# The half swaps of the rotary embedding: their transfers issued by GpSimd instead of ScalarE

## The chip, the cores and the metric

The kernel runs on one core of one Trainium2 chip. Time is the device time of one execution in microseconds (us). The engines named here are TensorE (PE, matrix products; PEld is its weight load), VectorE (DVE, elementwise work and reductions), ScalarE (ACT, activations and copies), GpSimd (POOL) and SyncE (SP, which here only issues DMAs). Each engine runs its own list of instructions in order; semaphores tie the lists together. A DMA is issued from an engine's list and moves its data afterwards, on 16 DMA engines that all queues share.

## The reference

Two pre-norm layers over 512 tokens of width 1024, all in float32, and a final RMSNorm. Each layer projects the normalised input to 23 chunks of 128 columns and feeds them to two groups of heads:

```
h = rmsnorm(x, g); z = h @ w_in
u_lru, g_lru, q, g_nsa, kc, vc, ks, vs, kwn, vwn, gate_logits = split(z)
y_lru = rg_lru(causal_depthwise_conv(u_lru))               # gated linear recurrence over the tokens
o_cmp = cmp_attention(q, compress(kc), compress(vc))       # compressed branch, q not rotated
q_rot = apply_rope(q)
o_slc = slc_attention(q_rot, apply_rope(ks), vs)           # selected blocks (here all 8 of them)
o_win = win_attention(q_rot, apply_rope(kwn), vwn)
y = [y_lru * silu(g_lru), (gated sum of the three o) * silu(g_nsa)]
x = x + y @ w_out

def apply_rope(t):                                          # per head of 64: halves x1, x2 of 32
    return concat(x1*cos - x2*sin, x2*cos + x1*sin)
```

`apply_rope` needs, beside each row of a chunk, the row of the other half of its head.

## The kernel before

Everything is kept transposed: a chunk of a projection is a tile of 128 columns (partitions) by 512 tokens. A weight chunk is loaded by SP into one of four `stage` slots, split by ACT into a high part `w_hi` (L774) and by DVE into a low part `w_lo` (L983), and PE multiplies it in 8 pieces of three matmuls (L1351 to L1353) into one of three PSUM banks. DVE takes the bank out, times `rstd`, into one of six slots of `E` (step EV: L1032, for q chunks L1029).

The order of all steps of a layer is written out in `schedule()`, and each engine walks through that one list and does its own part of each step, so it is the order on every engine. Six chunks of a layer are rotated: ks, kw and q0 to q3. For each the list has

- SWAP: four DMAs (L837) copy blocks of 32 partitions of the chunk in `E` into the slot `n % 2` of `swp` with the two halves of each head exchanged. ACT issues them; it first waits for EV of that chunk, and for the rotation two chunks earlier to be done with the slot. In the second layer the first of them also waits until the squares of the norm, which use `swp` too, are added up.
- ROPE: DVE waits until all four have landed, then multiplies `swp` by `sinT` (L1217), `E` by `cosT` (L1218) and adds them (L1219).
- RHI and LOW: ACT copies the result to `q_st` or `k_st` (L895), DVE stores the remainder (L1229).

For the q chunks the order on DVE is EV q(n), then the low part of a weight chunk, `cmpb` (CMPE, L1205, of the chunk before), ROPE q(n), and right behind it EV q(n+1). On PE the step CMP (L1576, scores of the compressed branch) of q(n) stands in the middle of the projection of chunk n+1 and waits for EV q(n); after q3 the step TURN (L1568) of the gate chunk waits in the same manner for the EV of `gate`, which stands behind ROPE q3.

GpSimd builds constants in the first 4 us, computes roots (L749, L762), and adds the squares between the layers (L738, L741); it has nothing to do while the chunks are projected.

Of the kernel before, what the change touches and what calls it, by code (L numbers as in the profile page):

```python
# [35 lines left out]
KT = D_MODEL // P  # L36
# [13 lines left out]
N_STAGE, N_RING, N_PT, N_E, N_SWP = 4, 3, 3, 6, 2  # L50
# [326 lines left out]
def hybrid_trunk(nc, x, norm_g, w_in, conv_w, conv_b, lru_wa, lru_ba, lru_wi, lru_bi, lru_lambda,  # L377
# [3 lines left out]
    plan = Plan(sched)  # L381
    split_no, load_no, z_no, aux_no, e_no = plan.split_no, plan.load_no, plan.z_no, plan.aux_no, plan.e_no
    rope_no, unit_no, turn_no, data_no, group_no = plan.rope_no, plan.unit_no, plan.turn_no, plan.data_no, plan.group_no

    ctx = ExitStack()
    with ctx:
        def sb(name, shape, dt=F32):
            return ctx.enter_context(nc.sbuf_tensor(name, shape, dt))

        def sem(name):  # L390
            return ctx.enter_context(nc.semaphore(name))
# [20 lines left out]
        swp = sb("swp", [P, N_SWP, SEQ])  # L412
# [48 lines left out]
        z_full, z_dve = sem("z_full"), sem("z_dve")  # L461
# [10 lines left out]
        squared, sq_added, root_ok, diag_ok = sem("squared"), sem("sq_added"), sem("root_ok"), sem("diag_ok")  # L472
# [6 lines left out]
        rot_ok, rope_hi, rope_lo, swapped = sem("rot_ok"), sem("rope_hi"), sem("rope_lo"), sem("swapped")  # L479
# [31 lines left out]
        def e_slot(key):  # L511
            return E[:, e_no[key] % N_E, :]
# [186 lines left out]
        @block.gpsimd  # L699
        def _(pool):  # L700
            links = [0]

            def link(ins):

                links[0] += 1
                ins.then_inc(pool_link, 1)
                pool.wait_ge(pool_link, links[0])

            link(pool.memset(ident[:, :], 0.0))
            link(pool.affine_select(out=ident[:, :], in_=ident[:, :], compare_op=ALU.not_equal, fill=1.0,  # L710
                                    base=0, pattern=[[-1, P]], channel_multiplier=1))
            pool.memset(ones[:, :], 1.0).then_inc(first_consts, 1)
            pool.tensor_copy(ident_b[:, :], ident[:, :]).then_inc(consts, 1)
            pool.tensor_tensor(fold[:, :], ident[:, 0:NCOL], ident[:, NCOL:2 * NCOL], ALU.add).then_inc(consts, 1)
            link(pool.memset(causal_b[:, :], 0.0))

            pool.affine_select(out=causal_b[:, :], in_=causal_b[:, :], compare_op=ALU.is_ge, fill=BIG, base=0,
                               pattern=[[-1, P]], channel_multiplier=1).then_inc(consts, 1)
            link(pool.memset(mask_c[:, :, :], 0.0))

            pool.affine_select(out=mask_c[:, :, :], in_=mask_c[:, :, :], compare_op=ALU.is_ge, fill=BIG,
                               base=-(CMP_LEN - 1), pattern=[[P, TT], [-CMP_STRIDE, NC]],
                               channel_multiplier=1).then_inc(consts, 1)
            link(pool.memset(row_ok[:, :], 1.0))

            pool.affine_select(out=row_ok[:, :], in_=row_ok[:, :], compare_op=ALU.is_ge, fill=0.0,
                               base=-(CMP_LEN - 1), pattern=[[P, TT]], channel_multiplier=1).then_inc(consts, 1)
            pool.memset(kc_bd[:, :], 0.0).then_inc(consts, 1)
            pool.memset(mhalf[:, :], -0.5).then_inc(consts, 1)
            pool.memset(upad[:, 0:CONV_W - 1], 0.0).then_inc(consts, 1)  # L730
            pool.wait_ge(consts, N_CONST)

            def add_square(tag, m):

                n = tag * KT + m
                pool.wait_ge(squared, n + 1)
                if m == 0:
                    pool.tensor_copy(sq_acc, sq_tmp).then_inc(sq_added, 1)  # L738
                else:
                    pool.wait_ge(sq_added, n)  # L740
                    pool.tensor_tensor(sq_acc, sq_acc, sq_tmp, ALU.add).then_inc(sq_added, 1)  # L741

            def root(tag):

                if tag < 0:
                    pool.wait_ge(x_mean, 1)
                else:
                    pool.wait_ge(a_dve, plan.freed(plan.aux, aux_no[("ss", tag)])[1])
                pool.tensor_tensor(rt[:, :], ms[:, :], mhalf[:, :], ALU.pow).then_inc(root_ok, 1)  # L749

            root(-1)
            for st in sched:
                kind = st[0]
                if kind == "ON":
                    for m in (2 * st[2], 2 * st[2] + 1):
                        add_square(st[1], m)
                elif kind == "NORM":
                    root(st[1])
                elif kind == "FMEAN":
                    t = st[2]  # L760
                    pool.wait_ge(fin_mean, t + 1)
                    pool.tensor_tensor(fin_rt[:, t:t + 1], fin_ms[:, t:t + 1], mhalf[:, 0:1], ALU.pow).then_inc(fin_root, 1)  # L762

        @block.scalar
        def _(act):
# [24 lines left out]
            def evicted(l, name):  # L790
                act.wait_ge(z_dve, plan.freed(plan.z, z_no[("Z", l, name)])[1])
# [19 lines left out]
            for st in sched:  # L811
                kind = st[0]
# [11 lines left out]
                if kind == "TANH":  # L824
                    _, l, name = st
                    evicted(l, name)
                    act.activation(silu_g[:, int(name[-1]), :], e_slot((l, name)), ACT.Tanh, scale=0.5).then_inc(gate_tanh, 1)
                elif kind == "SWAP":
                    _, l, name = st
                    n = rope_no[(l, name)]  # L830
                    evicted(l, name)
                    if n >= N_SWP:
                        act.wait_ge(rot_ok, n - N_SWP + 1)
                    if name == "ks" and l >= 1:
                        act.wait_ge(sq_added, KT * l)
                    for a in range(4):
                        act.dma_start(swp[32 * a:32 * a + 32, n % N_SWP, :],  # L837
                                      e_slot((l, name))[32 * (a ^ 1):32 * (a ^ 1) + 32, :]).then_inc(swapped, 16)
                elif kind == "GATES":
                    _, l, t = st  # L840
                    n = CT * l + t
# [16 lines left out]
                elif kind == "SQRT":  # L858
                    _, l, half = st
# [3 lines left out]
                elif kind == "YH" and st[2] == "n":  # L863
                    _, l, _, i = st
# [4 lines left out]
                elif kind == "YH":  # L869
                    _, l, t = st  # L870
# [4 lines left out]
                elif kind == "FLAT":  # L875
                    _, l, kv = st
# [9 lines left out]
                elif kind == "RHI":  # L886
                    _, l, name = st
# [9 lines left out]
                elif kind == "TURNE":  # L897
                    _, l, name = st
# [12 lines left out]
                elif kind == "S":  # L911
                    _, l, unit, r = st
# [11 lines left out]
                    for g in range(N_KV):  # L924
                        n, j = 4 * u + 2 * r + g, 2 * g + r
# [4 lines left out]
                elif kind == "T":  # L930
                    key = (st[1], *st[2])
                    if key[1] != "B" and data_no[key] % 2 == 0:
                        n, d, rows = turn_no[key], data_no[key], P if key[1] == "P" else NC
# [4 lines left out]
                    elif key[1] == "B":  # L938
                        l, _, i, b = key
# [11 lines left out]
                elif kind == "GE":  # L951
                    _, l, t, c = st
# [664 lines left out]
```

## Time and profile before

| | us |
|---|---|
| median of 3 runs | 629.15 (627.08 to 630.05) |
| the profiled execution: its own time | 629.98 |
| the profiled execution: span from first to last instruction | 628.3 |
| PE busy | 584.3 (93%) |
| DVE busy | 402.6 (64%) |
| ACT busy | 294.1 (47%) |
| POOL busy | 16.0 (3%) |

The 1.7 us between span and time lie outside the recorded instructions. The mean granted clock of TensorE is 0.985 of full speed. Issuing a DMA isn't counted as busy, though the engine's list stands still for it: 48 swap transfers are issued by ACT at 0.61 us each, about 29 us of its list. The first layer projects from about 12 to 150 us, the second from about 335 to 460 us; between and behind them PE works on attention and on the output projection.

### The profile page before, as it was taken

What the parts mean: (1) busy time and instruction counts of PE and PEld (TensorE: products, weight loads), DVE (VectorE), ACT (ScalarE), POOL (GpSimd) and SP (SyncE); (2) the same over time, 40 slices, a digit from 0 to 9 for tenths busy, and PEclk for the clock granted to TensorE, in tenths of its full rate; (3) what the DMA queues carried; (4) which work ended last, traced back from release to release, by engine and by line L of the source; (5) the groups of instructions that cost most, each with busy time, mean ns of one, the idle gap of its engine ahead of it and who ended that gap; (6) DMA issues with size and microseconds to landing.
All of it is one profiled execution on the core that took longest, in us unless ns stands there. A gap on an engine that the chain in (4) does not pass through costs nothing.

```text
span 628.3 us, 8688 instructions
## 1 busy us (share of the span) xinstructions
PE 584.3 (93%) x3207; PEld 409.1 (65%) x3207; DVE 402.6 (64%) x690; ACT 294.1 (47%) x586; POOL 16.0 (3%) x32
## 2 busy tenths in 40 slices
PE   4999999889999989998999999999899999999994
PEld 3776777667556555555788677777776666555563
DVE  4786966776555664755576679667664766557532
ACT  3647654424444452543453574462344545445522
POOL 1000000000000000000230000000000000000000
PEclk9999999998999998999899999998999999999999
DMA  8755393343111110101232745734421112000112
GB/s 243 201 155 152 87 231 85 84 102 104 56 34 34 34 35 1 34 0 35 67 101 70 198 122 145 142 82 99 110 74 35 34 39 64 0 2 1 34 34 68
DMA packets 94889, 50.71 MB, mean 81 GB/s; under 512 B 42992, under 2 KB 92288, under 8 KB 94848
## 3 DMA queue, kind: packets, MB, share of 16 engines
q1 hardware_dynamic: 91456, 45.95, 28.9%
q10 hardware_dynamic: 3392, 4.21, 2.5%
q8 instruction: 26, 0.43, 0.3%
q14 instruction: 15, 0.12, 0.1%
HBM read 44.90 MB, written 2.10 MB: 75 GB/s over the span
## 4 chain that ended last, share of the span: by engine, by line
PE 65%; DVE 13%; ACT 8%; DMA 5%; issue 5%; ACTq 2%; POOLq 0%; POOL 0%; DVEq 0%
PE z_ps L1351 10%; PE z_ps L1353 9%; PE z_ps L1352 9%; PE s_ps L1410 6%; PE t_ps L1426 5%; PE a_ps L1462 5%; DMA swp<-E 4%; PE o_ps L1462 3%; ACTq L837 2%; PE o_ps L1351 2%; PE o_ps L1352 2%; PE o_ps L1353 2%; ACT probs L928 2%; PE s_ps L1413 2%; DVE w_lo L983 2%
## 5 line engine op out<-in xcount | busy, mean ns | idle before, releaser
L1351 PE MATMUL z_ps<-h_hi,w_hi 128*128 128x512 f32 x264 | 111.1, 421 | 3.1 <-DVE h_lo L976 2.2
L928 ACT ACTIVATE probs<-s_ps,mn 128x128 f32<-128x128 f32 (+3 forms) x128 | 66.3, 523 | 99.7 <-DVE mn L1259 87.5
L1353 PE MATMUL z_ps<-h_hi,w_lo 128*128 128x512 f32 x264 | 103.6, 393 | 0.0
L1352 PE MATMUL z_ps<-h_lo,w_hi 128*128 128x512 f32 x264 | 103.6, 392 | 0.0
L774 ACT ACTIVATE w_hi<-stage 128x1024 fp32r<-128x1024 f32 x58 | 61.0, 1054 | 74.2 <-PE z_ps L1353 44.8
L1259 DVE TENSOR_REDUCE mn<-s_ps 128x1 f32<-128x128 f32 (+3 forms) x128 | 56.8, 485 | 52.0 <-PE s_ps L1413 51.9
L983 DVE TENSOR_TENSOR w_lo<-stage,w_hi 128x1024 fp32r<-128x1024 f32 x58 | 71.1, 1226 | 11.1 <-ACT w_hi L774 10.0
L1351 PEld LDWEIGHTS z_ps<-h_hi,w_hi 128*128 128x128 f32 x264 | 49.9, 189 | 22.4 <-issue 14.5
L1353 PEld LDWEIGHTS z_ps<-h_hi,w_lo 128*128 128x128 f32 x264 | 49.8, 189 | 11.1
L1267 DVE COPY probsT<-t_ps 128x512 f32<-128x512 f32 (+1 forms) x48 | 32.9, 686 | 36.1 <-PE t_ps L1426 24.8
L1352 PEld LDWEIGHTS z_ps<-h_lo,w_hi 128*128 128x128 f32 x264 | 50.1, 190 | 7.9 <-issue 0.2
L1410 PE MATMUL s_ps<-k_st,q_st 64*128 64x128 f32 (+3 forms) x384 | 47.2, 351 | 3.5 <-ACT probs L928 3.4
L1426 PE MATMUL t_ps<-ident,probs 128*128 128x128 f32 x320 | 49.3, 280 | 0.3 <-ACT probs L928 0.2
L1426 PEld LDWEIGHTS t_ps<-ident,probs 128*128 128x128 f32 x320 | 36.0, 141 | 15.3 <-issue 11.9
L1410 PEld LDWEIGHTS s_ps<-k_st,q_st 64*128 64x128 f32 x384 | 28.9, 187 | 24.5 <-issue 14.5
L937 ACT ACTIVATE probsT<-t_ps 128x512 f32<-128x512 f32 (+1 forms) x48 | 28.4, 592 | 34.9 <-PE t_ps L1426 34.8
L1351 PE MATMUL o_ps<-h_hi,w_hi 128*128 128x512 f32 x104 | 43.4, 417 | 0.0
L1353 PE MATMUL o_ps<-h_hi,w_lo 128*128 128x512 f32 x104 | 41.9, 403 | 0.0
L1352 PE MATMUL o_ps<-h_lo,w_hi 128*128 128x512 f32 x104 | 41.8, 402 | 0.0
L1462 PE MATMUL a_ps<-probsT,v_sb 128*64 128x256 f32 x192 | 30.9, 403 | 0.5 <-DVE probsT L1267 0.5
L1351 PE MATMUL z_ps<-y_hi,w_hi 128*128 128x512 f32 x64 | 31.0, 484 | 0.0
L1032 DVE TENSOR_TENSOR E<-z_ps,rstd 128x512 f32<-128x512 f32 x23 | 15.8, 689 | 19.3 <-PE z_ps L1353 17.3
(220 smaller groups left out, 904.0 us busy)
## 6 DMA issues: line engine op xcount, KB each, us to landing
stage<-in_w_in SPq DMA_DIRECT2D x28, 512.0 KB, 4.2
stage<-in_w_in SPq DMA_DIRECT2D x32, 256.0 KB, 4.0
stage<-in_cmp_k_w SPq DMA_DIRECT2D x8, 512.0 KB, 3.9
stage<-in_cmp_v_w SPq DMA_DIRECT2D x8, 512.0 KB, 5.0
stage<-in_w_out SPq DMA_DIRECT2D x8, 512.0 KB, 3.4
stage<-in_w_out SPq DMA_DIRECT2D x16, 256.0 KB, 3.9
swp<-E ACTq DMA_DIRECT2D x48, 64.0 KB, 2.1
out<-xT SPq DMA_DIRECT2D x8, 256.0 KB, 2.5
```

The costliest lines, as they stand in the source:

```text
L774: act.activation(split_into(n)[0], stage_of(key), ACT.Copy).then_inc(hi_split, 1)
L928: act.activation(probs[:, 4 * (u % 2) + j, 0:W], s_ps[g][:, 0:W], ACT.Exp, scale=-1.0, bias=mn[:, u % 2, j:j + 1], accum_out=rs[:, b, col: ...
L937: act.activation(probsT[0:rows, d % N_PT, :], t_ps[n % 2][0:rows, :], ACT.Copy).then_inc(pt_act, 1)
L983: dve.tensor_tensor(lo, stage_of(plan.split[n]), hi.bitcast(F32), ALU.subtract).then_inc(lo_dve, 1)
L1259: dve.tensor_reduce(mn[:, u % 2, j:j + 1], s_ps[g][:, 0:W], AX.X, ALU.min).then_inc(min_ok, 1)
L1267: dve.tensor_copy(probsT[0:rows, d % N_PT, :], t_ps[n % 2][0:rows, :]).then_inc(pt_dve, 1)
L1351: pe.matmul(bank, w_hi[:, slot, at:at + P], x_hi, start=first, stop=False)
L1352: pe.matmul(bank, w_hi[:, slot, at:at + P], x_lo, start=False, stop=False)
L1353: ins = pe.matmul(bank, w_lo[:, slot, at:at + P], x_hi, start=False, stop=last)
L1410: pe.matmul(s_ps[g][:, 0:W], q_st[rows, GROUP * of_q + at, i * P:(i + 1) * P], k_st[rows, b, of_k, 0:W], start=(part == 0), stop=False)
L1426: ins = pe.transpose(bank[:, j * P:(j + 1) * P], probs[:, 4 * (u % 2) + j, k * P:(k + 1) * P], ident[:, :])
L1462: ins = pe.matmul(o_bank(l, i, b)[g * HD:(g + 1) * HD, pair * N_PAIR_COL:(pair + 1) * N_PAIR_COL], v, probsT[0:rows, d % N_PT, g * 2 * P:( ...
```

## The change

The branch for SWAP is taken out of ACT's walk through the list and put into GpSimd's. The four transfers, their blocks, their semaphore and the waits in front are the same. DVE, PE and SP keep their instructions and their order.

```diff
@@ in GpSimd's program @@
                 elif kind == "NORM":
                     root(st[1])
+                elif kind == "SWAP":
+                    _, l, name = st
+                    n = rope_no[(l, name)]
+                    pool.wait_ge(z_dve, plan.freed(plan.z, z_no[("Z", l, name)])[1])
+                    if n >= N_SWP:
+                        pool.wait_ge(rot_ok, n - N_SWP + 1)
+                    if name == "ks" and l >= 1:
+                        pool.wait_ge(sq_added, KT * l)
+                    for a in range(4):
+                        pool.dma_start(swp[32 * a:32 * a + 32, n % N_SWP, :],
+                                       e_slot((l, name))[32 * (a ^ 1):32 * (a ^ 1) + 32, :]).then_inc(swapped, 16)
@@ in ScalarE's program @@
-                elif kind == "SWAP":
-                    _, l, name = st
-                    n = rope_no[(l, name)]
-                    evicted(l, name)
-                    if n >= N_SWP:
-                        act.wait_ge(rot_ok, n - N_SWP + 1)
-                    if name == "ks" and l >= 1:
-                        act.wait_ge(sq_added, KT * l)
-                    for a in range(4):
-                        act.dma_start(swp[32 * a:32 * a + 32, n % N_SWP, :],
-                                      e_slot((l, name))[32 * (a ^ 1):32 * (a ^ 1) + 32, :]).then_inc(swapped, 16)
```

ACT's list before, where q1 and q2 of the first layer are swapped (L774 is the high part of a weight chunk, L874 a copy for the recurrence, L895 the copy of a rotated chunk):

```order
L774 ACTIVATE w_hi<-stage 128x1024
L874 ACTIVATE y_hi<-probs 128x512
L837 DMA swp<-E 32x512 x4
L774 ACTIVATE w_hi<-stage 128x1024
L895 ACTIVATE q_st<-E 128x512
L837 DMA swp<-E 32x512 x4
```

The same place after the change (line numbers shift by 11 down to the removed branch):

```order
L785 ACTIVATE w_hi<-stage 128x1024
L874 ACTIVATE y_hi<-probs 128x512
L785 ACTIVATE w_hi<-stage 128x1024
L895 ACTIVATE q_st<-E 128x512
L874 ACTIVATE y_hi<-probs 128x512
L785 ACTIVATE w_hi<-stage 128x1024
```

The two groups of four DMAs are gone from ACT, and nothing else moved. GpSimd's list from the first root on, before and after:

```order
 L749 TENSOR_TENSOR rt<-ms,mhalf 128x4
+L768 DMA swp<-E 32x512 x24
 L738 COPY upad<-swp 128x512
 L741 TENSOR_TENSOR upad<-upad,swp 128x512 x7
 L749 TENSOR_TENSOR rt<-ms,mhalf 128x4
+L768 DMA swp<-E 32x512 x24
```

The 24 DMAs of a layer are six groups of four; the first of each group waits for the EV of its chunk. They stand alone between GpSimd's other work, so a group starts when its chunk is ready.

## Rows read from the trace of the kernel before

**Rows 1.** The page, part 1: busy time of each engine, share, instructions.
```profile
PE 584.3 (93%) x3207; PEld 409.1 (65%) x3207; DVE 402.6 (64%) x690; ACT 294.1 (47%) x586; POOL 16.0 (3%) x32
```
**Rows 2.** The page, part 4: the chain that ended last, by engine.
```profile
PE 65%; DVE 13%; ACT 8%; DMA 5%; issue 5%; ACTq 2%; POOLq 0%; POOL 0%; DVEq 0%
```
**Rows 3.** Waits of PE, 40 to 460 us: us in total, times, longest.
```profile
PE s_ps L1576 <- DVE E L1029: 4.0, 3, 1.4
...
PE a_ps L1568 <- DVE E L1032: 3.2, 2, 1.6
...
PE a_ps L1576 <- DVE E L1029: 2.4, 2, 1.2
...
PE t_ps L1521 <- DVE probs L1141: 1.1, 2, 0.7
PE s_ps L1558 <- DVE hid L1188: 1.0, 1, 1.0
```
**Rows 4.** Waits of DVE in the whole span, the rotations' own.
```profile
DVE swp L1217 <- DMA swp<-E: 19.4, 9, 3.4
```
**Rows 5.** The chain in order of time, round q1: start, us, what.
```profile
116.04 0.69 DVE E L1029
116.75 0.51 ACTq L837
...
118.58 3.23 DMA swp<-E
...
121.93 0.69 DVE swp L1217
```
**Rows 6.** Line 837, the four swap transfers of q1: time to landing.
```profile
DMA to landing us min/median/max: 1.9/2.1/3.2
```
**Rows 7.** Stretches with PE busy, clock, DMA share at the end: one microsecond each.
```profile
121.00:122.00 1.00, 1.00 (x6) 0.84 (x5) 0.07 (x1) 0.84 (x1) 0.00 (x0) 1.00 1.28 271
...
123.00:124.00 1.00, 0.41 (x2) 0.00 (x0) 0.96 (x3) 0.01 (x1) 0.00 (x0) 1.00 0.00 0
```
**Rows 8.** POOL's timeline: start, us, line, operation.
```profile
3.88 0.10 POOL L730 MEMSET upad<- 128x3 f32 x1
24.82 1.03 POOL L749 TENSOR_TENSOR rt<-ms,mhalf 128x4 f32<-128x4 f32 x1 [20.85 <-DVE ms L1085]
...
309.14 1.65 POOL L741 TENSOR_TENSOR upad<-upad,swp 128x512 f32<-128x512 f32 x1 [2.36 <-ACT swp L784]
```
**Rows 9.** Timeline of DVE and ACT round ks of the first layer.
```profile
49.42 0.68 DVE L1032 TENSOR_TENSOR E<-z_ps,rstd 128x512 f32<-128x512 f32 x1
...
51.10 2.52 ACTq L837 DMA_DIRECT2D swp<-E  x4
...
53.72 0.68 ACT L850 ACTIVATE probsT<-t_ps,hba 64x512 f32<-64x512 f32 x1 [2.25 <-issue]
...
59.42 0.69 DVE L1217 TENSOR_TENSOR swp<-swp,sinT 128x512 f32<-128x512 f32 x1 [0.30 <-DMA swp<-E]
```
**Rows 10.** The same round kw of the first layer.
```profile
66.35 2.44 ACTq L837 DMA_DIRECT2D swp<-E  x4
...
72.06 0.68 DVE L1217 TENSOR_TENSOR swp<-swp,sinT 128x512 f32<-128x512 f32 x1
```
**Rows 11.** Line 837, the four swap transfers of kw: time to landing.
```profile
DMA to landing us min/median/max: 1.9/2.1/3.5
```
**Rows 12.** Stretches of one q chunk in each layer, columns as in 7.
```profile
124.60:132.60 8.00, 6.63 (x32) 5.32 (x32) 7.27 (x11) 2.22 (x4) 0.00 (x0) 1.00 0.46 100
...
430.80:438.90 8.10, 8.07 (x32) 6.54 (x33) 7.33 (x11) 2.36 (x4) 0.00 (x0) 0.79 0.48 97
```
**Rows 13.** Timeline of DVE while q1's swap is issued.
```profile
116.89 0.69 DVE L1170 TENSOR_TENSOR y_lo<-probs,y_hi 128x512 fp32r<-128x512 f32 x1 [0.17 <-ACT y_hi L874]
117.50 1.22 DVE L983 TENSOR_TENSOR w_lo<-stage,w_hi 128x1024 fp32r<-128x1024 f32 x1
```

## The prediction

> **What bounds the kernel now.** I read the busy shares first. PE is at 93%, ACT at 47%, POOL at 3% [rows 1]. That points to PE, and says that taking work off ACT is worth nothing in most places. The chain of waits says where it isn't PE: 65% of it is PE, 13% DVE, 5% DMA and 2% the issuing of DMAs by ACT [rows 2]. The last two are the part that this change touches, so I looked for the place where they lie, in PE's waits during the two projections. PE waits three times for 4.0 us and twice for 2.4 us at L1576 and twice for 3.2 us at L1568, all for DVE's evictions of q1 to q3 and of the gate chunk [rows 3]: 9.6 us in seven waits. DVE in turn waits nine times, 19.4 us in all, for swap transfers [rows 4]: all four q chunks of each layer and ks of the first.
>
> The chain round q1 shows the loop: the eviction of q1 starts at 116.04 and takes 0.69, ACT issues the first transfer at 116.75, the last leaves at 118.58 and takes 3.23 to land, the rotation starts at 121.93 [rows 5]. Behind the rotation's three instructions stands the eviction of q2, for which PE waits and behind which the next swap is issued. One turn takes 8.0 us, in which PE has 6.63 us of work [rows 12]. So from q0 on the stage runs at the pace of DVE and the swap, not of PE. The leg from the end of the eviction (116.73) to the rotation is 5.2 us; whatever it gains or loses goes into the end, until PE is the limit again.
>
> **What is removed.** ACT loses twelve groups of four issues of 0.61 us. In the q loop this buys nothing on ACT itself: it had no other work that DVE or PE waited for there. What it could buy is an earlier start, and there is none: ACT issued 0.02 us after the eviction of q1 ended [rows 5]. At ks of the first layer there is one: the eviction ended at 50.10 and ACT came to it at 51.10, behind other work, and its gate activations stood 2.25 us behind the issues [rows 9]. Without them the hidden layer of the compression comes earlier, and PE's wait of 1.0 us for it (L1558, one in each layer) shrinks [rows 3]. But behind it PE waits for DVE at L1521 (1.1 us in two waits) [rows 3], and DVE comes there from the rotation of ks. What PE gains at L1558 it waits at L1521, unless the swap of ks lands earlier too. I cost the relief at nothing, hidden by DVE.
>
> **What is added.** POOL issues the same transfers. It is idle all through both projections, so no group waits behind other work of POOL, and the order of the groups doesn't hold one back: the slot of `swp` is free long before. Two sizes are unknown, since no row shows a DMA issued by POOL.
>
> First, the distance between two issues. The same operation takes ACT 0.61 us (four in 2.44) [rows 10]. POOL's own instructions take from 0.10 us (a tiny memset) over 1.03 us (a root of 128x4, almost no data) to 1.65 us (an addition of 128x512) [rows 8]. The ends are 0.10 and 1.65. I take 1.03, the row for an instruction that is nearly all software on POOL. Three distances then cost 3 x (1.03 - 0.61) = 1.26 us per group, with ends of -1.5 and +3.1.
>
> Second, the landing. Of q1's four transfers most land in 2.1 us and the slowest in 3.2 [rows 6], which is the last. It overlaps the load of the next weight chunk, which SP issues when DVE has split the one before; the DMA engines are full at 121 to 122 us and idle by 123 to 124 [rows 7]. A transfer that leaves later still meets that load, but it can't be held up much beyond its end. Ends: 1.1 us less (it lands like the others) and 3.2 more (6.4, against 3.2, as ks has it under loads of its own: the rotation's start at 59.42 less the last issue at 52.99 [rows 9]). I take +0.25.
>
> The Trainium skill (DMA: Bandwidth & Descriptors, section on latency and other measured facts) puts the first byte at about 1 us for a DMA from GpSimd and 0.6 us for one from SP or ACT. By it the second term would be 0.4 and the sum 1.2 us larger; no run so far shows it.
>
> Summed up, for a group of four in the first layer, and the second by the same rows:
> - q0 to q3: 1.26 + 0.25 = 1.51 us on each leg. Each has DVE idle before the rotation and PE waiting behind it, so each counts in full: 8 x 1.51 = 12.1 us.
> - ks: POOL starts at 50.15, the last leaves at 50.15 + 3.09 = 53.24, against 51.10 + 3 x 0.63 = 52.99, so 0.25, and 0.25 for the landing: 0.5 in each layer, 1.0 together.
> - kw: the last left at 68.18 and landed 3.5 later, at 71.7 [rows 10, 11]; the rotation came at 72.06, kept by other work of DVE. With 1.51 more it lands at 73.2, 1.15 late. DVE is what PE waits for at L1521 behind it, so this counts: 2.3 for both layers.
>
> Together 15.4 us, on the profiled execution's own 629.98: 645.4. The median of the runs lies 0.8 below that execution, so 644.5.
>
> TensorE's clock: in one turn of the q loop of the second layer it was granted 0.79 of full speed on the mean, which is part of the stretch at its lower level of 1.2 GHz, after turns in which PE had waited for DVE [rows 12]. With longer waits there may be more of it, but PE has then 8 to 9.5 us for 6.63 us of work, so the loop hides most of it. I leave it out of the sum.
>
> **Rivals.**
> 1. POOL issues as quickly as ACT. Then only the landing is left, 0 to 0.25 on each of 12 groups: 0 to 3 us, 629 to 632. For it speaks that it is the same instruction with as few bytes; against it the root's 1.03 us for 512 numbers [rows 8], which says that POOL spends long on little.
> 2. Faster: POOL's issues are much shorter than ACT's, down to the 0.10 of the memset. The last transfer then leaves 1.5 us earlier, ahead of SP's load, and lands in 2.1 in place of 3.2. The leg shrinks by 2.6 us, PE becomes the limit, and what can be won is PE's seven waits, 9.6 us: 619.5. It decides in favour of faster as soon as the distance is under 0.61 with the landing kept. Against it: it needs an issue to cost no more than the smallest memset, while the root, with hardly any data, takes ten times that [rows 8].
> 3. POOL can't work on a transfer while DVE runs. DVE starts 1.9 us of instructions with two inputs from SBUF right behind the eviction of q1 (0.69 and 1.22) [rows 13]. If these hold POOL up, each leg is 1.9 longer: 12 x 1.9 = 22.8 on top of 15.4, 667; if only partly, 655 to 667. POOL's additions, 1.65 once, are a sign that it can be slowed.
>  The Trainium skill (SBUF — State Buffer, section on its two separate sides) has such a rule, and it speaks against this change: GpSimd is locked out of the port pair that it shares with VectorE while VectorE runs an operation in a two-port mode, an fp32 copy from SBUF to SBUF for one, and cannot write descriptors then; an operation with two SBUF inputs blocks it only where it reads SBUF. By that wording the q legs would be spared; this trace shows neither.
>
> **How the numbers follow.** The sum with its own spread 0.62, rival 1 0.14, rival 2 0.07, rival 3 0.17. What this kernel's measurement can tell from no change is 0.5%, 3.1 us: 626.0 to 632.3. Faster by more: 0.07, rival 2. Within: 0.08, most of rival 1. Slower: 0.85. The sum's own spread goes from a distance of 0.75 (about 635) to 1.65 (8 x (3.12 + 0.25) = 27.0, and some 5 for ks and kw: about 662). The range for 8 in 10 is 632 to 664: it takes in part of rivals 1 and 3.
>
> **What would show it.** In the profile after: issues under POOL's queue with their mean against 1.03 us; DVE's wait at L1217 grown from 19.4 us to about 33, and twelve waits or nearly so; PE's seven waits at L1576 and L1568 grown by about 12 us; ACT's idle time "issue" before L850 gone, with PE's wait at L1558 smaller and that at L1521 larger. I am wrong in the mechanism if the legs are longer and PE's waits aren't; wrong in size if the distance is off 1.03 or the last transfer lands much later than 3.5 us after its issue.

## The result, and the profile after

| | before | after |
|---|---|---|
| median of the runs (us) | 629.6 (627.1 to 635.3, 4 runs) | 620.4 (617.1 to 621.8, 4 runs) |
| ratio to before, 95% interval | | 0.986 (0.983 to 0.990) |
| profiled execution / its span (us) | 629.98 / 628.3 | 621.83 / 620.1 |
| mean granted clock of TensorE | 0.985 | 0.986 |

The change makes the kernel 7 to 9 us faster. The forecast was 644.5, with 0.07 on faster. The same kernel measured again among the experiments gave 620.4 and 0.988 (0.983 to 0.994). So the direction was wrong, and I start with the view that priced it: the source line of the transfers on POOL, in the stretch of q1 of the first layer (duration min/median/max in ns, first and last start in us, then the landing).

```profile
L768 POOL DMA_DIRECT2D swp<-E x4: 496/497/498, 116.3 to 117.8; - x4
...
DMA to landing us min/median/max: 1.8/1.9/2.0
```

Four issues stand within 1.96 us: a distance of 0.49, where I had put 1.03 and ACT had 0.61. And the slowest of the four lands in 2.0, where it took 3.2 before [rows 6]. The chain of waits after, round q1 (start, us, what), to be laid beside [rows 5]:

```profile
115.34 0.69 DVE E L1029
116.03 0.28 issue
116.31 1.31 POOL swp L768 x3
117.62 0.15 issue
117.78 1.89 DMA swp<-E
119.79 0.69 DVE swp L1217
```

Read it from the end of the eviction (116.03). POOL takes 0.28 to start, where ACT took 0.02 [rows 5]. The three distances take 1.47, where ACT's took 1.83. So the last transfer leaves 1.76 behind the eviction, before 1.85: 0.1 us won. The landing then is 1.89, before 3.23: 1.34 won. The leg from the eviction to the rotation goes from 5.21 to 3.77, and nearly all of it is landing.

Of the page, the busy shares answer to [rows 1] and the chain by engine to [rows 2]: POOL has 48 instructions and 24 us more, PE is the same, and DMA in the chain falls from 5% to 3%.

```profile
PE 582.4 (94%) x3207; PEld 408.2 (66%) x3207; DVE 402.8 (65%) x690; ACT 293.9 (47%) x586; POOL 40.0 (6%) x80
...
PE 65%; DVE 17%; ACT 8%; issue 5%; DMA 3%; POOL 1%; POOLq 0%; DVEq 0%; ACTq 0%
```

What that transfer meets is in the timelines (start, us, line, operation), first after, then before: the last of the four issues, and the first issue of the load of the next weight chunk. SP's starts 0.33 us behind the start of POOL's, and 0.23 behind that of ACT's. By their ends POOL's is 0.20 ahead of SP's, and ACT's 0.02 behind it.

```profile
117.78 0.50 POOL L768 DMA_DIRECT2D swp<-E  x1
118.11 0.37 SPq L636 DMA_DIRECT2D stage<-in_w_in  x1
```
```profile
118.58 0.62 ACTq L837 DMA_DIRECT2D swp<-E  x1
118.81 0.37 SPq L636 DMA_DIRECT2D stage<-in_w_in  x1
```

The three turns from the end of q1's eviction to that of the gate chunk, in each layer, before and after (length, busy us and count of PE, PEld, DVE, ACT, POOL, granted clock, DMA share, GB/s):

```profile
116.72:140.84 24.12, 19.91 (x96) 15.96 (x96) 17.34 (x26) 5.60 (x8) 0.00 (x0) 1.00 0.46 99
422.76:447.05 24.29, 21.30 (x96) 17.13 (x96) 17.34 (x25) 5.70 (x8) 0.00 (x0) 0.93 0.47 97
```
```profile
116.02:137.34 21.32, 19.69 (x96) 15.98 (x96) 17.25 (x26) 5.60 (x8) 5.88 (x12) 1.00 0.52 112
416.86:437.11 20.25, 19.40 (x96) 15.98 (x96) 17.24 (x25) 5.60 (x8) 5.88 (x12) 1.00 0.55 117
```

The same 96 matmuls of each layer take 48.4 us in all before and 41.6 after, 6.8 less; PE has about 39 us of work in them at full clock, so there are 2.5 us left to win. The waits of PE in the two projections (us in total, times, longest) answer to [rows 3]:

```profile
PE a_ps L1576 <- DVE E L1029: 2.0, 2, 1.2
PE s_ps L1576 <- DVE E L1029: 2.0, 2, 1.2
PE t_ps L1521 <- DVE probs L1141: 1.7, 2, 1.2
PE a_ps L1568 <- DVE E L1032: 0.8, 1, 0.8
```

PE's seven waits of 9.6 us behind DVE's evictions are five of 4.8. Its waits at L1558, 1.0 in each layer, are gone, and that at L1521 grew from 1.1 to 1.7. DVE's wait for the swaps fell from 19.4 us in nine [rows 4] to:

```profile
DVE swp L1217 <- DMA swp<-E: 11.6, 7, 2.2
```

Where the whole difference arises, from the ends of the evictions in the two profiled executions (us gained, sum so far in brackets):

| stretch | first layer | second layer |
|---|---|---|
| to ks | 0.15 (0.15) | 0.25 lost from that eviction to ks (4.82) |
| ks to q0 | 0.49 (0.64) | 1.06 (5.88) |
| q0 to q1 | 0.06 (0.70) | 0.02 (5.90) |
| q1 to the gate chunk | 2.80 (3.50) | 4.04 (9.94) |
| gate chunk to the eviction behind it | 1.57 (5.07) | 1.74 lost to the end (8.20) |

Behind the q turns the clock has a share. Stretches of 4 us of before, and the same of after (columns as above):

```profile
140.00:144.00 4.00, 3.10 (x12) 2.55 (x13) 2.67 (x4) 0.63 (x1) 0.00 (x0) 0.77 0.14 31
144.00:148.00 4.00, 4.00 (x20) 2.89 (x19) 2.07 (x4) 2.03 (x2) 0.00 (x0) 0.80 0.73 198
432.00:436.00 4.00, 4.00 (x12) 3.13 (x12) 3.61 (x5) 0.62 (x1) 0.00 (x0) 0.57 0.76 164
```
```profile
140.00:144.00 4.00, 4.00 (x24) 3.05 (x23) 2.77 (x6) 3.09 (x7) 0.00 (x0) 1.00 0.78 213
432.00:436.00 4.00, 4.00 (x19) 3.28 (x18) 2.99 (x6) 1.06 (x1) 0.97 (x2) 1.00 0.91 192
604.00:608.00 4.00, 2.60 (x10) 2.18 (x11) 1.09 (x2) 1.25 (x2) 0.54 (x1) 0.76 0.43 124
```

Before, PE was granted 0.57 to 0.80 at these places, part of each stretch at 1.2 GHz in place of 2.4; after the change it has full clock there. The 1.57 us behind the gate chunk of the first layer are all clock: the same 25 matmuls keep PE busy for 5.69 us at a granted 0.70 before (140.84 to 146.59) and for 4.11 at 1.00 after. They aren't tied to the length of the waits in the turns: the same stretch takes 4.15 in e9 and e14, whose turns are longer than those of before. The drop at 604 of after, where the trace of before has none, stands in the last stretch of the table, which loses 1.74. The exact gain of a single pair of executions is therefore to be read with some 2 us of play.

### The profile page after: what moved, and what is told of

It is laid out like the page before. It is cut to its first block, busy times and chain, and to the rows that moved or that the text cites. A ratio compares the mean times of both kernels' runs of the same rounds, so it can differ in the third digit from the quotient of the medians.

```text
span 620.1 us, 8688 instructions
## 1 busy us (share of the span) xinstructions
PE 582.4 (94%) x3207; PEld 408.2 (66%) x3207; DVE 402.8 (65%) x690; ACT 293.9 (47%) x586; POOL 40.0 (6%) x80
## 3 DMA queue, kind: packets, MB, share of 16 engines
q10 hardware_dynamic: 1088, 1.06, 0.6%
## 4 chain that ended last, share of the span: by engine, by line
PE 65%; DVE 17%; ACT 8%; issue 5%; DMA 3%; POOL 1%; POOLq 0%; DVEq 0%; ACTq 0%
PE z_ps L1351 10%; PE z_ps L1353 9%; PE z_ps L1352 9%; PE s_ps L1410 7%; PE t_ps L1426 6%; PE a_ps L1462 5%; PE o_ps L1462 3%; DVE w_lo L983 3%; DMA swp<-E 2%; ACT probs L928 2%; PE s_ps L1413 2%; PE o_ps L1351 2%; PE o_ps L1353 2%; PE o_ps L1352 2%; DVE probs L1157 2%
## 5 line engine op out<-in xcount | busy, mean ns | idle before, releaser
L1352 PEld LDWEIGHTS z_ps<-h_lo,w_hi 128*128 128x128 f32 x264 | 50.1, 190 | 7.8 <-issue 0.2
L1351 PE MATMUL o_ps<-h_hi,w_hi 128*128 128x512 f32 x104 | 42.2, 405 | 0.0
L768 POOL DMA_DIRECT2D swp<-E x48 | 24.0, 507 | 189.3 <-DVE E L1029 112.5
```

Source lines behind the costliest of these rows:

```text
L1351: pe.matmul(bank, w_hi[:, slot, at:at + P], x_hi, start=first, stop=False)
L1352: pe.matmul(bank, w_hi[:, slot, at:at + P], x_lo, start=False, stop=False)
```

## The experiments

Ratios are to the kernel before on the same chip, with 95% intervals. "Turns" is the length of the six turns above, both layers, in the profiled execution.

| kernel | median (us) | ratio | turns (us) | leg of q1, first layer |
|---|---|---|---|---|
| before | 628 to 630 | 1 | 48.4 | 5.21 |
| after | 620.4 | 0.986 (0.983 to 0.990) | 41.6 | 3.77 |
| e1 only q by POOL | 620.9 | 0.985 (0.979 to 0.991) | 42.0 | 3.87 |
| e2 only ks, kw by POOL | 626.3 | 0.996 (0.992 to 1.000) | 49.0 | 5.29 |
| e3 ACT issues, load held | 620.3 | 0.983 (0.977 to 0.989) | 42.2 | 4.03 |
| e4 POOL issues, load held | 619.4 | 0.981 (0.973 to 0.989) | 41.3 | 3.75 |
| e5 root between issues | 650.5 | 1.033 (1.027 to 1.039) | 60.0 | 7.64 |
| e6 ACT kept busy | 621.9 | 0.989 (0.984 to 0.995) | 41.7 | 3.75 |
| e7 two each | 619.9 | 0.983 (0.976 to 0.989) | 39.4 | 3.2 |
| e8 two each, load held | 618.2 | 0.983 (0.977 to 0.988) | 39.2 | 3.21 |
| e9 memset between issues | 647.4 | 1.029 (1.022 to 1.037) | 57.7 | 6.88 |
| e10 tiny memset ahead | 618.1 | 0.983 (0.977 to 0.990) | 41.0 | 3.6 |
| e11 after, again | 620.4 | 0.988 (0.983 to 0.994) | 41.5 | 3.77 |
| e12 e8, again | 619.9 | 0.986 (0.981 to 0.990) | 39.2 | 3.21 |
| e13 linked memset of 8 columns ahead | 623.1 | 0.993 (0.989 to 0.996) | 43.8 | 3.97 |
| e14 linked memset of 384 columns ahead | 630.9 | 1.005 (1.001 to 1.009) | 50.1 | 5.56 |

### Which groups carry the gain (e1, e2)

The groups of transfers are split by name. In e1 POOL issues those of q and ACT the others, in e2 it is the other way round. Those that stay on ACT have a semaphore of their own.

```diff
+        def by_pool(name):
+            return (0, 1, 2, 3) if stem(name) == "q" else ()
...
-                elif kind == "SWAP":
+                elif kind == "SWAP" and by_pool(st[2]):
```

> Only the swaps of q0 to q3 are issued by GpSimd, those of ks and kw by ScalarE as before (a semaphore for each issuer). Theory A: the gain is the shorter leg from eviction to rotation at the eight q chunks, where PE waits. Then this keeps at least 6.5 of the 8.2 us that the profiled spans of before and after differ by: span about 621 to 622. Theory B: the gain comes from ScalarE's freed list, which other work of ScalarE waits behind only at ks and kw. Then this gains little, 0 to 2 us: span about 626 to 628.

> The other half: only ks and kw are issued by GpSimd, q0 to q3 by ScalarE. Theory A: 0 to 2 us faster than before, span 626 to 628, with PE's wait for the hidden layer (L1558) gone and given back at PE's next wait for DVE (before, L1521 waited 1.1 us). Theory B: 6 us or more faster, span under 623.

e1 has the whole gain (0.985), e2 has 0.996 with an interval that reaches to 1.000. The q groups carry it. (The profiled execution of e2 was its longest, 633.5, so its span says nothing against the expectation.) Beyond the turns there is a small part on ks: from the eviction of ks to that of q0 it takes 50.5 us before in each layer, 50.7 and 50.5 in e1, 50.0 and 49.5 in e2, 50.0 and 49.5 after. So what comes with ks and kw leaving ACT is some 1.5 us in all.

### Is it the issuer or the load (e3, e4)

SP waits with the load of a weight chunk until the swaps that stand before it in the list have landed. In e3 ACT issues the transfers as before, in e4 POOL does.

```diff
+        def swaps_before(n):
+            at = [p for p, st in enumerate(sched) if st[0] in ("LO", "ON")]
+            return sum(st[0] == "SWAP" for st in sched[:at[n - N_RING]]) if n >= N_RING else 0
...
                         wait_low(sync, split_no[old])
+                        if swaps_before(split_no[old]):
+                            sync.wait_ge(swapped, 64 * swaps_before(split_no[old]))
```

> As before, ScalarE issues all swaps, but SyncE issues a weight load only when the swap that stands before it in the list has landed. Theory C: the last of ScalarE's four transfers lands late (3.2 to 3.7 us in place of 2.0) since it reaches the queues of the DMA engines together with SyncE's load; GpSimd's comes ahead of it. Then here all four land in 2.0 to 2.2 us, the q legs shrink from 5.2 to 4.0 us, and 5 to 8 us of the gain are had with ScalarE as issuer: span 620 to 623. Theory D: a transfer issued by GpSimd lands sooner by itself, whatever SyncE does. Then the last still takes over 3 us here and the span stays at 627 to 630.

> The changed kernel with the same hold of SyncE's loads. Theory C: only q0 (slowest landing 3.4 us after the change) and q3 of the first layer (3.0) still met a load; with the hold they land in 2.0 too and the span falls by 1 to 2 us against the changed kernel (618 to 619), unless the weight loads, started later, come late. Theory D: nothing changes, 619 to 621. What it has over the same hold with ScalarE as issuer is then the difference of issuing alone: 3 x (0.61 - 0.49) less 0.26 of later start, 0.1 us for a group, under 1 us in all.

With ACT as issuer and the load out of the way the kernel is as fast as after (0.983 against 0.986). The chain of e3 round q1:

```profile
116.30 0.69 DVE E L1036
...
117.01 0.51 ACTq L844
...
118.84 2.05 DMA swp<-E
...
121.01 0.69 DVE swp L1224
```
```profile
120.98 0.99 SPq L643 DMA_DIRECT2D stage<-in_w_in  x2
```

ACT's issues are as long as ever (the last leaves 1.85 behind the eviction), the landing is 2.05 in place of 3.23, and the load is issued at 120.98, behind it. Nothing but the load moved, and the leg fell from 5.21 to 4.03. On the new kernel the same hold adds next to nothing at q1 (3.75 against 3.77): there is no delay left to take away there. I had expected 1 to 2 us from q0 and from q3 of the first layer, whose last transfers still land late after the change (3.4 and 3.0). With the hold q0's leg falls from 5.30 to 3.75, and in e3 from 6.61 to 4.03, and the way from q0's eviction to q1's stays at 16.03 in both: q0's leg is worth nothing. q3's last transfer lands as late as before the hold (2.9), so what it meets there isn't the weight load.

### The price of a longer distance, and DVE beside POOL (e5, e9)

e5 puts a root of one column between the transfers of a group. e9, made because the distance of e5 came out uneven, puts a memset of 384 columns there instead. The lines of both, one below the other:

```diff
                     for a in range(4):
+                        if a:
+                            at = 3 * n + a - 1      # e5
+                            pool.tensor_tensor(spin[:, at:at + 1], mhalf[:, 0:1], mhalf[:, 0:1], ALU.pow)
+                            link(pool.memset(spin[:, :], 0.0))      # e9, in its place
```

> The changed kernel with a root of one column (0.54 to 0.57 us on GpSimd) between each two of the four transfers, which brings their distance from 0.49 to about 1.03 us, what the prediction had taken. If the prediction failed only in that size, this gives what it forecast: 3 x 0.54 = 1.6 us more on each leg than after the change and the last transfer under SyncE's load again (1.2 more), 8 x 1.6 to 2.8 = 13 to 22 us on the changed kernel: span 633 to 642, slower than before. If legs don't count in full (the model of the loop is wrong), it stays under 630.

> The changed kernel with a linked memset of 128x384 on GpSimd between each two transfers, for a distance near 1.0 us (the roots of the run before came to 1.1 and, beside VectorE's two-input work, once in a group to 2.1). The prediction's model with the prediction's distance: each of the eight q legs near 1.5 us over before (5.2 to 5.4 becomes 6.7 to 6.9), span about 640 to 648. If legs don't count in full, it stays nearer to 630.

Both are slower, 1.033 and 1.029, e5 by more than expected, since one root of each group made a distance of 2.1 us at q1 in place of 1.1. POOL's timeline of e9 in q1's group (start, us, what, in brackets the idle time before it and what ended it):

```profile
121.34 0.50 POOL L771 DMA_DIRECT2D swp<-E  x1 [12.55 <-DVE E L1032]
121.83 0.44 POOL L770 MEMSET spin<- 128x384 f32 x1
122.56 0.50 POOL L771 DMA_DIRECT2D swp<-E  x1 [0.29 <-POOL spin L770]
...
```

A distance of 1.22 (0.50 + 0.44 + 0.29) gives 647.4, near the 644.5 that I had forecast for 1.03. Of the profiled pair's 11.1 us (639.4 less 628.3) the six turns are 9.3, and the six legs in them grew by the same 9.3 (1.67, 1.81 and 1.32 in the first layer; 1.60, 1.63 and 1.31 in the second). So the model of the loop holds for q1 to q3. kw's rotation comes at 6.83 and 6.77 behind its eviction in place of 5.74, 1.1 and 1.0 late, near the 1.15 that I had forecast for 1.03. The total is near by luck: q0's leg didn't count as forecast (its way to q1 grew by 0.6 and 0.0), the last transfers landed in 2.8 to 3.1 at q1 to q3 where I had 3.5, and from ks to q0 5.5 us came where I had 3.3, part of them clock (0.97 granted in both layers in place of 1.00). Two of e9's turns show the clock in them:

```profile
121.05:130.55 9.50, 8.25 (x32) 6.47 (x32) 4.74 (x8) 1.69 (x3) 3.27 (x7) 0.82 0.37 84
...
140.36:149.97 9.61, 9.56 (x32) 7.73 (x32) 5.34 (x8) 1.69 (x3) 3.27 (x7) 0.67 0.37 84
```

PE waits more, is granted 0.67 of full speed in one turn of 9.6 us, part of it at 1.2 GHz, and is busy 9.56 us with what takes 6.63 otherwise [rows 12]: the turn hides it only just, and so it adds nothing to the turns, which grew as the legs did.

e5 tells of the third rival. POOL beside DVE, in the timelines of e5 (POOL, then DVE):

```profile
122.58 1.61 POOL L771 TENSOR_TENSOR spin<-mhalf 128x1 f32<-128x1 f32 x1
...
124.73 0.57 POOL L771 TENSOR_TENSOR spin<-mhalf 128x1 f32<-128x1 f32 x1
```
```profile
122.55 1.22 DVE L987 TENSOR_TENSOR w_lo<-stage,w_hi 128x1024 fp32r<-128x1024 f32 x1
```

The same root takes 1.61 beside DVE's instruction with two inputs from SBUF and 0.57 when that is over. It reads SBUF. In the kernel after, the issues of the transfers stand beside the same instruction and take 0.50 each:

```profile
116.31 1.96 POOL L768 DMA_DIRECT2D swp<-E  x4 [14.07 <-DVE E L1029]
```
```profile
116.80 1.22 DVE L983 TENSOR_TENSOR w_lo<-stage,w_hi 128x1024 fp32r<-128x1024 f32 x1
```

### Does ACT's relief count (e6)

ACT runs four linked copies of 128x512 where it issued the group before.

```diff
+                elif kind == "SWAP":
+                    evicted(*st[1:])
...
+                    for a in range(4):
+                        spun = 4 * rope_no[st[1:]] + a + 1
+                        act.activation(spin[:, :], cosT[:, :], ACT.Copy).then_inc(act_spun, 1)
+                        act.wait_ge(act_spun, spun)
```

> The changed kernel, and ScalarE at each swap runs four copies of 128x512 (0.6 us each, linked, about 2.7 us) into a tile that nobody reads, so that its list stands still about as long as when it issued the transfers. Theory A (legs): the span stays within 1.5 us of the changed kernel's 620. Theory B (ScalarE's list): it goes back by 6 us or more, over 626.

The time (0.989, 0.984 to 0.995) can't be told from that of after. The stretches can: from ks to q0 it takes 50.6 and 50.8 us, as before (50.5), and not 50.0 and 49.5 as after, while the turns stay at 41.7. This agrees with e1 and e2: ACT's relief is worth about 1.5 us, on ks alone, and nothing in the q turns.

### Sharing the group (e7, e8, e11, e12)

ACT issues two transfers of each group and POOL two; e8 holds the load back as well.

```diff
+        def by_pool(name):
+            return (2, 3)
+
+        def by_act(name):
+            return (0, 1)
```

> Two of the four transfers of each swap from ScalarE, two from GpSimd. By the legs: the last leaves 0.64 us (ScalarE) or 0.28 + 0.49 = 0.77 us (GpSimd) behind the eviction in place of 1.75, and lands 2.0 later: a leg of about 2.9 in place of 3.8. DVE has 2.3 us of other work in the leg of q1 and PE waits 4.8 us in all for the q chunks after the change, so 4 to 5 us more are had at the most: span 615 to 618. If the transfers bound the leg otherwise (the DMA engines themselves, 256 KB a swap), 619 to 620.

> The split between ScalarE and GpSimd, with SyncE's loads held until the swap before them has landed. Theory C: the transfers are out before the load anyway, except at q0, where the load of two chunks runs: within 1 us of the split without a hold, 614 to 618.

> The changed kernel once more, unchanged, beside the next one on one chip: 617 to 622, a ratio of about 0.986.

> The split between ScalarE and GpSimd with held loads, again, in more rounds. From the legs (3.2 us in place of 3.8 at q1, 3.2 in place of 5.3 at q0) it should beat the changed kernel by 2 to 3 us of PE's waits: 616 to 619, a ratio of about 0.981. If what is won there is given back behind it, the two are the same within 1 us.

All are issued 1.27 behind the eviction, the leg of q1 falls to 3.2, and the turns to 39.2, which is what PE has to do in them. e7 was expected at 615 to 618 and came at 619.9. The time doesn't follow beyond doubt: e8 and e12 give 0.983 and 0.986, after and e11 0.986 and 0.988, with intervals that overlap. The turns are 2.4 us shorter than after's, 0.4% of the time, while the times of one kernel are up to 9 us apart (616.0 to 624.7 in e11). If there is a better version, it is this one, by up to 2 us; these runs don't show it.

### How close the last transfer is to the load (e10, e13, e14)

A memset ahead of the group is to delay its start and nothing else: one column (e10, the first line below), 8 columns with a wait for its end (e13), 384 columns with that wait (e14, the second line).

```diff
+                    pool.memset(spin[:, n:n + 1], 0.0)
+                    link(pool.memset(spin[:, :], 0.0))
                     for a in range(4):
```

> The changed kernel with one memset of 128x1 on GpSimd ahead of each group, which puts the group 0.1 to 0.5 us later and leaves the distances at 0.49. Theory C (what decides is whether the last transfer is in the queues before SyncE's load, issued 2.1 us behind the eviction): the last one is now issued with or behind the load and lands in 3.0 to 3.5 us in place of 2.0, the legs of q1 and of q3 of the second layer grow by 1.3 to 1.7 us from 3.8, and 3 to 6 us of the gain are gone: span 623 to 627. Theory D (GpSimd's transfers land quickly by themselves): the legs grow by the delay alone, 0.1 to 0.5 us each, span 620 to 623.

> The changed kernel with a linked memset of 128x8 on GpSimd ahead of each group: GpSimd waits for its own memset and then issues, which should start the group 0.1 to 0.2 us later than after the change (at about 0.45 us behind the eviction; the last transfer leaves at 1.9, SyncE's load at 2.1). Theory C: the last transfer is then nearly level with the load, as ScalarE's was (1.86), and lands in 2.0 to 3.2; q legs of 4.0 to 5.3. Theory D: legs of 3.9 to 4.0 at q1.

> The same with a linked memset of 128x384 (0.44 us and 0.29 until the issue behind it): the group starts at about 0.8, the last transfer leaves at about 2.3, behind SyncE's load. Theory C: it lands in 3 us or more, the leg of q1 is 5.3 us or more (2.3 + 3.0), as long as before the change, and the time is 626 to 631. Theory D: the leg is 2.3 + 2.0 = 4.3, the time about 4 us over the changed kernel, 622 to 625.

e10 failed as a test: the group came earlier, not later. In POOL's timeline the memset starts 0.06 behind the eviction (116.28), and the first transfer at once, at 0.10, where it takes 0.28 when the transfer itself waits:

```profile
116.34 0.10 POOL L768 MEMSET spin<- 128x1 f32 x1 [14.04 <-DVE E L1031]
116.38 1.96 POOL L770 DMA_DIRECT2D swp<-E  x4
```

With the wait the delay is there. e13 starts its groups 0.46 behind the eviction, e14 0.78. The chain of e14 and its load:

```profile
116.36 0.69 DVE E L1031
117.11 0.43 POOL spin L768
...
119.28 3.19 DMA swp<-E
122.60 0.69 DVE swp L1219
```
```profile
119.13 1.00 SPq L637 DMA_DIRECT2D stage<-in_w_in  x2
```

The last transfer now leaves 0.15 behind the load and lands in 3.19, as it did when ACT issued it. A start 0.49 later than after's costs 1.79 on the leg of q1 (5.56 against 3.77), and the whole gain is gone (630.9; 50.1 us of turns against 48.4 before). e13, at 0.17 later, keeps the landings at q1 (1.9 and 2.0), its last transfer 0.15 ahead of the load (117.53 and 117.68), and loses that of q3 of the second layer (3.1 in place of 1.9); those of q0, late after the change already (3.4 and 3.5), come at 4.0 and 3.9. About half of the gain remains. By the starts of the issues the pairs at q1 are then: 0.33 ahead of the load 1.9, 0.15 ahead 1.9 to 2.0, 0.15 behind 3.2, all by POOL; and by ACT, 0.23 ahead, 3.2. At q1 it is a step, not a slope.

ACT's pair doesn't fit in by the starts, and it does by the ends. ACT's last issue takes 0.62 and ends 0.02 behind the end of the load's first issue (119.20 and 119.18), POOL's takes 0.50 and ends 0.20 ahead of it, and in e13 0.02 to 0.03 ahead. That it isn't a matter of ACT or its queue alone shows kw in e10, where in both layers an issue of POOL took 0.63: it starts 0.20 ahead of the load, ends 0.06 behind the end of the load's first issue, and lands in 3.2, as ACT's does. The two issues, and the landing of the first:

```profile
67.50 0.63 POOL L770 DMA_DIRECT2D swp<-E  x1
67.70 0.37 SPq L637 DMA_DIRECT2D stage<-in_w_in  x1
```
```profile
DMA to landing us min/median/max: 3.2/3.2/3.2
```

The same count over kw and q0 to q3 in the traces in which one engine issues the whole group, at distances as in before or after, and no load is held (before, after, e1, e2, e6, e10, e11, e13, e14), without q3 of the first layer: of 81 last transfers, 29 end their issue 0.02 us or more ahead of the end of the load's first issue, and all land in 1.85 to 2.20; 50 end 0.02 or more behind, and all land in 3.0 to 4.6; two are level, and landed in 1.9 and 3.1. At q3 of the first layer all land late, in 2.8 or more, ahead of the load or not, and with the load held too (2.7 in e3, 2.9 in e4).

## Why the prediction was wrong

**What bounds the kernel: right from q1 on.** I had it from q0 on, and q0's leg bounds nothing (see below). The stage from q1 to the gate chunk runs at the pace of eviction, swap and rotation. e3, e5, e9 and e14 reach the turns through that leg alone, and the turns follow in both directions (42.2, 60.0, 57.7 and 50.1 us against 48.4).

**The distance between issues: wrong size and sign, 1.35 us per group.** I took 1.03 from POOL's root, and it is 0.49. The step "the row for an instruction that is nearly all software on POOL" failed: a root says nothing of what POOL needs for a DMA. I had both ends (0.10 and 1.65) and chose by likeness in a word. ACT's own 0.61 for the same operation was at least as near. The start costs 0.26 that I had at nothing (0.28 against 0.02), and the three distances give back 0.36, together -0.1 against the +1.26 forecast.

**The landing: wrong sign, 1.6 us per group, and this decides.** I put +0.25, measured is -1.34 at q1. I had seen that the slowest transfer overlaps the load [rows 6, 7], and that a transfer later than ACT's meets the same load, but not asked how near its front edge ACT's last one stood: its issue started 0.23 us ahead of the load's and ended 0.02 behind it. With such a margin the term has no middle value at q1. It is about 0 if the group gets no earlier and -1.3 if it gets a little earlier. e3 and e14 show both sides of the edge by one change each. Over the eight q groups the last landing fell by 0.7 to 1.8 us.

**Each leg counts in full: right for q1 to q3, wrong for q0.** From before to after, the legs of q1 to q3 fell by 1.44, 0.54 and 0.80 us in the first layer and by 1.58, 0.59 and 1.86 in the second, 6.8 together, and the six turns by the same 6.8. q0's leg fell by 1.3 and 0.9 us (6.61 to 5.30, 6.25 to 5.36), and the way from q0's eviction to q1's stayed at 16.0 in both layers: other work ends last there. In e9 it took 16.7 in the first layer and 16.0 in the second, so a longer leg hardly counts there either. What I had no term for is how far a leg can fall. q2's can't fall under 4.83, as DVE has its other work before that rotation: no idle time is left in the timeline, and the turn is 7.44 in every fast version. q3's is 4.87 and 3.77, since its transfers land late in the first layer whatever the load does. q1's gave all that issue and landing gave: turns of 7.83 and 8.01 became 6.39 and 6.43, with PE busy for 6.33 of the 6.39 (first layer, q1 and q2):

```profile
116.02:122.41 6.39, 6.33 (x32) 5.33 (x32) 4.74 (x8) 1.69 (x3) 1.96 (x4) 1.00 0.58 124
122.41:129.85 7.44, 6.71 (x34) 5.33 (x32) 7.16 (x10) 2.21 (x4) 1.96 (x4) 1.00 0.49 107
```

So 12.1 us slower were forecast for the legs and 6.8 faster came.

**ks and kw: +3.3 forecast, nothing of it there.** ks is started by POOL 0.32 behind the eviction in place of ACT's 1.00, where I had 0.05, and its leg got shorter, 9.32 to 8.83. kw's rotation came 5.74 behind its eviction before and after: DVE's other work hides the swap, which I had noted, and only my 1.51 would have broken through (as e9's distance did).

**ACT's relief: nothing forecast, about 1.5 us measured** (e1, e2 and e6 by their stretches). PE's wait at L1558 went as described. The step that failed is the one behind it: "what PE gains at L1558 it waits at L1521". Only 0.6 us of the 2.0 (1.0 in each layer) came back there.

**The clock: left out.** That the turns hide it was right: in e9 they grew as the legs did, at a granted 0.67 and 0.82. Outside the turns it counts. In the direction that came it is a small gain in this pair of executions (1.57 us at 140 to 148), which no run ties to the change.

**The rivals.** The second, at 0.07, is what happened: the last transfer gets ahead of SP's load, the legs shrink, PE comes near to being the limit (busy 39.1 of 41.6 us in the turns; 619.5 forecast, 620.4 measured). The mechanism is this rival's; that the number is so near is luck. Of the 9.6 us of PE's waits that it spent only 4.8 were won; 1.4 more came from the waits at L1558 less what L1521 gave back, and 1.9 from less busy time of PE (584.3 to 582.4). Its condition, "a distance under 0.61 with the landing kept", was right too. Against it I had put that an issue must cost no more than the smallest memset. That was false by the numbers of this trace: the last issue started only 0.1 us earlier than ACT's and ended 0.2 earlier, not 1.5. A rival with a step in it is to be weighed by its threshold, and I weighed it by its extreme. The first rival failed in that POOL was quicker, not as quick. The third is refuted: issues beside DVE's two-input work take 0.50 like the others. Beside DVE's fp32 copies from SBUF to SBUF some were longer, by little and not always. At kw of the first layer one took 0.72 us beside four such copies (first POOL, then DVE); at the same place in the second layer one took 0.50 (last line), with the same four copies from 368.24 on.

```profile
67.42 0.72 POOL L768 DMA_DIRECT2D swp<-E  x1
```
```profile
67.38 1.34 DVE L573 COPY cmpb<-E 64x248 f32<-64x248 f32 x4
```
```profile
368.27 0.50 POOL L768 DMA_DIRECT2D swp<-E  x1
```

Of that rival's two halves, the Trainium skill (SBUF — State Buffer, section "SBUF: two separate sides") states both: a DVE operation with two SBUF inputs shuts out only a GpSimd operation that reads SBUF, and a two-port copy shuts out GpSimd altogether. The root of e5 (1.61 against 0.57) and the issues (0.50) agree with the first. The second the runs don't settle: 0.72 and, in both layers of e10, 0.63 would agree with it, and 0.50 beside the same copies shows no hold-up, but each copy is so short (0.37) that it ends within the issue. The other page of the Trainium skill that the prediction weighed (DMA: Bandwidth & Descriptors, section "Latency and other measured facts") puts the first byte at about 1 us from GpSimd and 0.6 from the others. No run here shows a first byte; to the landing, POOL's transfers show nothing of the 0.4 us between them: undisturbed they land 1.8 to 2.0 us behind their issue from POOL and 1.9 to 2.1 from ACT.

**What stays open.** The end of the last issue against that of the load's first issue sorts the landings, but no run varied it alone, and why it should be the end isn't shown. Nor was it measured whether the load delays the transfer in the queues or in the memory. What q3's transfers of the first layer meet, with the load held too, is open as well; the DMA rows of that stretch have one packet of queue q8 (instruction) in before, after, e3 and e4, and in the second layer none, and nothing tests whether it matters.

## What to carry to other kernels

Before pricing a change that shifts a small transfer, look in the timeline at the distance between its issue and that of the next large load, by their ends as well as their starts: when it is a few tenths of a us, the term is a step of the whole collision (1.3 us here), and the cheapest remedy may be to hold the load (e3) and not to change the issuer. Price an unknown operation of an engine by the same operation on another engine rather than by another operation on the same engine. Take a leg as counting only where the next step waits for its end (three of the four q legs here), and a shortened one only down to what else stands before its consumer (q2's gave 0.5 us where q1's gave 1.4).

## What the runs showed of the hardware

- A DMA of 32x512 fp32 took POOL 0.49 to 0.50 us to issue and ACT 0.61 (the first of a group 0.51). The first that POOL issued in a layer took longer, 0.68 in the first layer and 0.56 in the second, at ks (after, e2) and at q0 where that was the first (e1). POOL starts 0.28 to 0.31 behind the event that it waits for, ACT 0.02 to 0.04.
- A memset that takes over the wait (e10) brought POOL's first transfer from 0.28 to 0.10 us behind the event. A memset with a wait for its own end puts 0.29 between the two.
- A small transfer landed in 1.85 to 2.20 us where its issue ended 0.02 us or more ahead of the end of the first issue of a large load on another queue, and in 3.0 to 4.6 where it ended 0.02 or more behind (29 and 50 cases, in nine traces, q3 of the first layer left out). By the starts alone 0.15 ahead was early enough for POOL at q1 (e13), and 0.20 ahead too late at kw (e10).
